# Starting the first gated head inside the last state-space group, and reordering the state steps of every group

## The reference, cut to what matters

```
xs, bm, cm = silu(dwconv(xbc))                       # state-space branch: 4 groups of 8 heads, 2 directions
y  = ssd_scan(xs, dt, a, bm, cm) + xs * d_skip       # chunks of 128 tokens: diagonal part + carried states
ys = rms_norm(y * silu(z), g_ssm_norm)               # norm over one group of 512 columns

lb = softmax(hg_lb)[0]                               # gated branch: 8 heads, 2 directions
log_f = log(lb + (1 - lb) * sigmoid(f));  k = (1 - lb) * sigmoid(-f);  q = silu(q)
o  = gla_scan(q, k, v, log_f)                        # cumulative gates, intra-chunk products, carried states
oh = rms_norm(o, g_hg_norm) * silu(og)

mixed = sigmoid(gm) * (ys @ w_branch_ssm) + sigmoid(gh) * (oh @ w_branch_hg)
```

## Time and profile before

| | |
|---|---|
| median of 3 runs | 2017.88 us (2017.27 to 2020.76) |
| profiled execution, its own time | 2020.66 us |
| its span | 2018.3 us |
| PE busy | 1781.8 us (88%) |
| DVE, ACT, POOL busy | 729.9, 449.8, 397.5 us |
| granted TensorE clock, mean | 0.955 of full speed |

### The profile page before, as it was taken

One profiled execution on the slowest core, in us unless ns is written; L12 is line 12 of the kernel. 1 busy time (PEld: TensorE's weight loads), 2 busy tenths in 40 slices (PEclk: granted clock), 3 DMA queues, 4 the chain that ended last, 5 costly groups with the idle time before them and its releaser, 6 DMA issues.

```text
span 2018.3 us, 18573 instructions
## 1 busy us (share of the span) xinstructions
PE 1781.8 (88%) x7064; PEld 963.0 (48%) x7064; DVE 729.9 (36%) x1148; ACT 449.8 (22%) x716; POOL 397.5 (20%) x464
## 2 busy tenths in 40 slices
PE   6899999999996999999999999998478878777782
PEld 1455555555554777677765444443423323333330
DVE  1534635455345665556665322124400000000003
ACT  2231231413224443434443000002110000000001
POOL 0103223141317443354441000000010000000000
PEclk9999999999998999999999999999589989899996
DMA  7212321322320111111132725212679999999993
GB/s 278 81 34 78 122 56 45 112 57 68 94 63 22 52 42 42 52 39 44 42 104 87 257 94 187 94 60 89 264 289 428 431 429 430 430 429 429 430 404 153
DMA packets 153554, 350.25 MB, mean 174 GB/s; under 512 B 14065, under 2 KB 104394, under 8 KB 140442
## 3 DMA queue, kind: packets, MB, share of 16 engines
q1 hardware_dynamic: 135962, 325.34, 42.8%
q10 hardware_dynamic: 12496, 15.75, 2.3%
q0 software_dynamic: 5040, 8.40, 1.1%
HBM read 346.09 MB, written 13.32 MB: 178 GB/s over the span
## 4 chain that ended last, share of the span: by engine, by line
PE 71%; DMA 19%; DVE 4%; POOL 3%; issue 2%; ACT 1%; SPq 0%; ACTq 0%; POOLq 0%; DVEq 0%
PE bank L498 10%; PE bank L709 10%; PE bank L747 6%; PE bank L2186 5%; PE bank L1702 5%; PE bank L1279 4%; PE bank L503 4%; DMA arena<-in_w_up_dram 3%; DMA stay<-in_w_up_dram 3%; DMA stay<-in_w_gate_dram 3%; PE bank L1704 3%; PE bank L1721 3%; PE bank L2204 3%; PE bank L494 3%; PE bank L1315 2%
## 5 line engine op out<-in xcount | busy, mean ns | idle before, releaser
L709 PE MATMUL bank<-stay,arena 128*128 128x512 f32 (+1 forms) x704 | 242.7, 501 | 9.9 <-DVE arena L934 7.7
L2186 PE MATMUL bank<-arena 128*64 128x512 f32 x832 | 201.3, 640 | 51.2 <-DMA arena<-in_w_up_dram 35.1
L709 PEld LDWEIGHTS bank<-stay,arena 128*128 128x128 f32 x704 | 133.5, 192 | 111.4 <-issue 101.3
L498 PE MATMUL bank<-arena 128*128 128x512 f32 x384 | 169.0, 593 | 1.5 <-ACT stay L610 1.5
L2186 PEld LDWEIGHTS bank<-arena 128*64 128x64 f32 x832 | 70.9, 147 | 180.1 <-issue 178.5
L2248 DVE TENSOR_TENSOR arena<-arena,bank 128x512 f32<-128x512 f32 x17 | 11.7, 688 | 325.8 <-PE bank L2186 325.8
L747 PE MATMUL bank<-arena,stay 128*128 128x512 f32 x256 | 114.0, 596 | 1.4 <-DVE arena L973 1.4
L1158 POOL TENSOR_TENSOR arena<-arena 128x256 f32<-128x256 f32 x112 | 86.6, 773 | 131.7 <-DVE arena L1472 117.5
L498 PEld LDWEIGHTS bank<-arena 128*128 128x128 f32 x384 | 71.7, 190 | 85.4 <-issue 85.4
L1471 DVE TENSOR_TENSOR arena<-arena 128x256 f32<-128x256 f32 x112 | 63.5, 607 | 132.0 <-ACT arena L1214 100.6
L2101 POOL DMA_INDIRECT y_dram<-arena x17 | 17.1, 1008 | 445.1 <-DVE arena L2255 444.5
(11 more groups left out here) (372 smaller groups left out, 2678.4 us busy)
## 6 DMA issues: line engine op xcount, KB each, us to landing
arena<-in_w_gate_dram SPq DMA_DIRECT2D x26, 2048.0 KB, 25.5
arena<-in_w_up_dram SPq DMA_DIRECT2D x26, 2048.0 KB, 26.9
arena<-in_w_down_dram SPq DMA_DIRECT2D x24, 2048.0 KB, 27.5
arena<-in_w_in_dram SPq DMA_DIRECT2D x58, 512.0 KB, 3.9
arena<-in_w_ada_dram SPq DMA_DIRECT2D x12, 2048.0 KB, 10.9
stay<-in_w_down_dram SPq DMA_DIRECT2D x10, 2048.0 KB, 26.0
stay<-in_w_gate_dram SPq DMA_DIRECT2D x8, 2048.0 KB, 25.7
stay<-in_w_up_dram SPq DMA_DIRECT2D x8, 2048.0 KB, 28.2
```

The source lines that it names most:

```text
L498: mm = pe.matmul(b[:, :], w[:, k, :], src[:, k, 0:LAT], start=(k == 0), stop=(k == KT - 1))
L709: mm = pe.matmul(ps[:, 0:n], w[:, k, :], hT[:, k, o:o + n], start=(k == 0), stop=(k == KT - 1))
L2186: mm = pe.matmul(b[cols, :], xgT[r][:, k, cols], w[u][:, k, :], start=(k == 0), stop=(k == KT - 1))
```

## The change

It has four parts.

1. **Every group.** POOL makes decayed x k = 3 ahead of exponents 3, 4 ahead of 4, and so on. State 9 moves from step 7 to step 6 on PE, and the two halves of the z projection (`gate(g, 3)`) now stand one ahead of state 8 and one ahead of state 9. In step 7 `off` 4 and 5 stand ahead of the diagonal.
2. **Groups 0 and 1.** ACT issues the two transfers of B and C weights (L422, L423) behind the last two x copies (L599), not ahead of them.
3. **Last group and head 0.** The bounds (`lower_bounds`, `lower_bound_terms`, `bounds`) move from the start of the gated branch into DVE's steps 0 and 5, ACT's exponential of them into step 3. ACT runs head 0's gates (`head_gates`) once the last diagonal is done, ahead of y's squares. PE runs units 0 and 1 of head 1 ahead of `turn_y` and unit 2 behind it. POOL starts the masks after the last `off`. Buffers are laid out anew so that nothing overlaps: the bounds get 69 columns of their own.
4. **Head bodies.** Head 0 is written out ahead of the loop; in it unit 3 stands behind level 0, and units 0 to 2 are gone (they ran before). In the other heads unit 1 moves from behind the key transposes to ahead of them, the wait for y's copies moves to those transposes, POOL does both end differences behind level 0's subtractions, and ACT does both end exponentials behind `rstd` and copies unit 1 ahead of the keys.

```diff
-        STATES = [(0,), (1, 2), (), (3, 4), (5,), (6, 7), (8,), (9,)]
+        STATES = [(0,), (1, 2), (), (3, 4), (5,), (6, 7), (8, 9), ()]
...
+        def head_gates(act, h, before):
+            act.wait_ge(s_pev, START + 8 * h + 5)
+            act.wait_ge(s_b, START + 2 * h)
+            for d in range(2):
+                act.activation(lf[d], pf[d], ACT.Sigmoid)
+            if before is not None:
+                output_sigmoid(act, before)
+            act.wait_ge(s_lw, START + NL * h)
+            for d in range(2):
+                act.activation(kh[d], pf[d], ACT.Sigmoid, scale=-1.0).then_inc(s_sg, 1)
+            act.activation(qh, pq, ACT.Sigmoid).then_inc(s_sg, 1)
+            act.preload_act_table_set(LOG_EXP)
+            act.wait_ge(s_lbh, h + 1)
+            act.wait_ge(s_sg, 4 * h + 3)
+            for d in range(2):
+                act.activation(lf[d], lf[d], ACT.Ln, scale=omlh[:, d:d + 1], bias=lbh[:, d:d + 1]).then_inc(s_ln, 1)
+
+        def output_sigmoid(act, h):
+            act.wait_ge(s_pev, START + 8 * h + 6)
+            act.wait_ge(s_q, h + 1)
+            act.activation(sog, pog, ACT.Sigmoid).then_inc(s_sg, 1)
...
+                decayed(3)
                 exponents(3)
-                for h in range(3, HG):
-                    if h < HG - 1:
-                        exponents(h + 1)
-                    for k in STATES[h]:
-                        decayed(k)
+                decayed(4)
+                exponents(4)
+                decayed(5)
+                exponents(5)
+                decayed(6)
+                decayed(7)
+                exponents(6)
+                decayed(8)
+                exponents(7)
+                decayed(9)
 
...
+                            if last and (h, part) == (3, 0):
+                                act.wait_ge(s_lbd, 1)
+                                act.activation(lbt[:, :], lbt[:, :], ACT.Exp).then_inc(s_lbe, 1)
...
+                    act.wait_ge(s_yd, START + HG * G)
+                    head_gates(act, 0, None)
                 for cc in range(LCH):
                     act.wait_ge(s_yz, START + 4 * g + cc + 1)
                     ins = act.activation(zs[:, cc, :], yt[:, cc, :], ACT.Square, accum_out=ssq[:, cc:cc + 1])
+                    if last and cc == 1:
+                        head_unit_copy(act, 0, 6)
                 ins.then_inc(s_ysum, 1)
-                act.preload_act_table_set(LOG_EXP)
+                if not last:
+                    act.preload_act_table_set(LOG_EXP)
                 act.wait_ge(s_ysum, 2 * g + 1)
...
+                    x_rows(g + 1, range(4, NCH))
                     if g + 2 < G:
                         bc_weights(act, g + 2)
-                    x_rows(g + 1, range(4, NCH))
...
-                    head_unit_copy(act, 0, 6)
                     head_unit_copy(act, 0, 7)
+                    head_unit_copy(act, 1, 0)
+                    head_unit_copy(act, 1, 1)
...
-                        if h > 2:
-                            gate(g, h // 2)
-                        for k in STATES[h]:
+                        for i, k in enumerate(STATES[h]):
+                            gate(g, h // 2, (i,) if h == 6 else (0, 1))
...
-                        state(g, 9)
                         off(g, 4)
+                        off(g, 5)
                         diagonal(g, h)
-                        for i in range(5, 8):
-                            off(g, i)
+                        off(g, 6)
+                        off(g, 7)
...
+                    head_unit(pe, 1, 0)
+                    head_unit(pe, 1, 1)
                     turn_y(g, True)
+                    head_unit(pe, 1, 2)
...
+                if last:
+                    lower_bounds(dve, own)
                 for h in range(1, HG - 1):
+                    if last and h == 5:
+                        lower_bound_terms(dve, own)
+                        bounds(dve, own, 0)
...
-            pool.wait_ge(s_yt, START + 16)
-            pool.wait_ge(s_yn, 16)
+            pool.wait_ge(s_yo, START + 8 * G)
...
+                    pool.wait_ge(s_yt, START + 4 * G)
...
-                end_differences(0)
                 pool.wait_ge(s_b, START + 2 * h + 2)
                 for i in range(NL):
                     if i == 1:
+                        end_differences(0)
                         end_differences(1)
...
-                end_exps(h, 0)
                 level_exp(h, 0)
                 if not first:
                     act.wait_ge(s_vc, h)
                     head_unit_copy(act, h, 7)
                     rstd(h - 1)
+                end_exps(h, 0)
...
-                if not last:
+                if first:
+                    head_unit_copy(act, h + 1, 2)
+                elif not last:
                     head_unit_copy(act, h + 1, 0)
+                    head_unit_copy(act, h + 1, 1)
                 else:
                     gate_copy(0, 0)
                     gate_copy(0, 1)
                 key_copies(h)
-                if not last:
-                    head_unit_copy(act, h + 1, 1)
                 level_exp(h, 2)
-                if not last:
+                if last:
+                    gate_copy(1, 0)
+                elif not first:
...
-            def body(h, last):
-                unit(h, last, 0)
+            def body(h, first, last):
+                if not first:
+                    unit(h, last, 0)
...
+                unit(h, last, 3 if first else 1)
+                if last:
+                    early_gate(pe, 1, 0, 0)
+                pe.wait_ge(s_ys, START + 4 * G)
...
-                unit(h, last, 1)
-                if last:
-                    early_gate(pe, 1, 0, 0)
                 level(h, 1)
-                unit(h, last, 2)
+                if not first:
+                    unit(h, last, 2)
```

More of the change, by code:

```diff
@@ L884, in ssd_tensor, with lower_bounds, lower_bound_terms, bounds @@
                 group(g)
+        def lower_bounds(dve, own):
+            a0, a1 = cols1[:, R_LB:R_LB + 16], cols1[:, R_LB + 16:R_LB + 32]
+            own.link(dve.tensor_tensor(lb, a0, a1, ALU.max))
+            own.mark(dve.tensor_tensor(lbt[:, 0:16], a0, lb, ALU.subtract))
+            dve.tensor_tensor(lbt[:, 16:32], a1, lb, ALU.subtract).then_inc(s_lbd, 1)
+        def lower_bound_terms(dve, own):
+            dve.wait_ge(s_lbe, 1)
+            own.wait()
+            own.link(dve.tensor_tensor(oml, lbt[:, 0:16], lbt[:, 16:32], ALU.add))
+            own.link(dve.reciprocal(oml, oml))
+            own.link(dve.tensor_tensor(lb, lbt[:, 0:16], oml, ALU.mult))
+            own.mark(dve.tensor_scalar(lb, lb, F_MIN, None, ALU.max))
+            own.mark(dve.tensor_tensor(oml, lbt[:, 16:32], oml, ALU.mult))
+            own.link(dve.tensor_copy(ghg, cols1[:, R_GHG:R_GHG + 1]))
+        def bounds(dve, own, h):
+            dve.wait_ge(s_ln, START + 2 * h)
+            own.mark(dve.tensor_copy(lbh, lb.rearrange("p (d h) -> p h d", d=2)[:, bass.ds(h, 1), :].rearrange("p a b -> p (a b)")))
+            dve.tensor_copy(omlh, oml.rearrange("p (d h) -> p h d", d=2)[:, bass.ds(h, 1), :].rearrange("p a b -> p (a b)")).then_inc(s_lbh, 1)
         def ssd_vector(dve, own):
@@ L1004, in group @@
                     weight(h + 1)
+                    if h == 6:
+                        keep_state(9)
                     if h % 2:
@@ L1349, in body @@
                 level(h, 2)
-                unit(h, last, 3)
+                if not first:
+                    unit(h, last, 3)
                 if last:
@@ L1495, in body @@
                 if not last:
-                    bounds(h + 1)
+                    bounds(dve, own, h + 1)
                 merge(0)
@@ L1533, in body @@
                     modulation_terms(dve, own, 0)
-            bounds(0)
             keys(0)
```

72 lines of the change are left out of this document (15 added, 57 removed).

## The result

| | before | after |
|---|---|---|
| median | 2019.32 us (2017.27 to 2021.93, 4 runs) | 1998.3 us (1996.2 to 2000.74, 4 runs) |
| ratio | | 0.9896, 95% interval 0.9877 to 0.9914 |
| profiled execution, span | 2018.3 us | 1993.7 us |
| granted clock, mean | 0.955 | 0.957 |
| unit 6 of head 0 starts | 596.24 us | 584.38 us |

The change makes the kernel 21.0 us faster, and 28.8 were forecast: 1989.1 us (1985.5 to 1996.5) against 1998.3 measured. The time lies outside the range. The mixer is 26.0 us shorter in the profiled pair, and the whole 24.6.

What follows compares the result with a forecast made beforehand. PE's row in the mixer was taken as the bound, its holes as all there is to win: 9.5 + 3.1 + 0.8 + 16.9 - 1.5 = 28.8 us off 2017.9 gives 1989.1 us, range 1985.5 to 1996.5.

Steps and rivals of the forecast that it cites:

- Decayed x, 9.5 us: Groups: PE's eight waits for decayed x, 7.9 us, plus 0.2 us start-up each, vanish; 9.5 us gained.
- State 9, 3.1: Step 6 of the groups: PE's waits for DVE's keeping of states shrink, with start-ups 3.1 us gained.
- the two transfers, 0.8: `turn_y`, where ACT issues two transfers ahead of its copies: 0.4 us saved, twice, 0.8 us.
- So the hole counts in full: Groups: no wait stands directly behind the removed ones, PE waits only 0.2 us at the z projection; 9.5 us kept.
- My own sign of being wrong: Listed as proof of error: gate(3) of a group, in the z projection, waiting over 0.5 us for DVE.
- The front, 16.9 us: Unit 6 to level 3 of head 0: 20.0 us over pure work vanish, 3.1 us of new wait; 16.9 us gained.
- The new hole ahead of level 2: Head 0: level 2's operand needs 4.1 us of hand-overs, level 1 covers 0.9; PE waits 3.1 us.
- the slow matmuls behind the 13 us hole: Front of head 0: matmuls after the hole ahead of level 0 ran slowly, 2.8 us together, counted as gain.
- The loop's debt, 1.5 us: Heads 1 to 6: level 1 waits for the later merge of the first product, 0.25 us each, 1.5 in all.
- The mixer, 28.8 us: Sum of all terms over groups, front and loop: the mixer gets 28.8 us shorter.
- the rivals: Full loop debt 1993.5 us (0.13), late front 1993 (0.13), groups without gain 2001.5 (0.08), slower 2030 (0.02), no change (0.02).
- So I take the gain off the median: Whole kernel: 28.8 us come off the median 2017.9, not off the profiled execution's time, 2.8 us above it.

Runs made afterwards that it cites:

- `pool_order`: Kernel before with one edit, GpSimd makes each decayed x ahead of the exponents of its step; 2012.21 us, ratio 0.9964.
- `states_only`: Kernel before with the rest of parts 1 and 2 (state 9 in step 6, transfers behind copies), GpSimd's order as before; 2020.12 us, ratio 0.9996.
- `best2`: Changed kernel; head 0's unit 3 between levels 1 and 2, first product merged first, GpSimd's exponents 5, 7 and 0 behind VectorE's steps; 1987.87 us.
- `warm`: Changed kernel with seven unread matmuls in the hole ahead of level 2 of head 0; 1995.97 us, ratio 0.9883.
- `again`: The changed kernel timed once more, unedited, in five rounds beside the kernel before; 1996.59 us, ratio 0.988.
- `fill`: Changed kernel with head 0's unit 3 between levels 1 and 2 instead of behind level 0; 1993.39 us, ratio 0.9868.
- `apart`: Changed kernel with GpSimd's exponents 5 waiting in every group until VectorE has multiplied weight 4; 1996.23 us, ratio 0.988.

## Why the prediction was wrong, by its own steps

- **Decayed x, 9.5 us**: right for what it removes (9.4 in `pool_order`). That full amount probably had luck in it: all six meetings of that trace went VectorE's way. **State 9, 3.1, and the two transfers, 0.8**: 2.6 for both together in `states_only`, where one new wait of 0.93 is in it; `turn_y` of group 1 takes 1.91 us (385.40) instead of 2.30, as forecast.
- **"So the hole counts in full"** is the first step that failed. Removing the waits is worth 14.0 us in `best2`, but the changed kernel gets 10.1 to 11.8: 1.5 to 3.2 us go into new waits for VectorE's `add_off`. My own sign of being wrong came true, the last quarter of a group's z projection waiting over 0.5 us for VectorE (0.83 at 217.93). I had worked out that VectorE's chain ends just when PE wants it, and gave it 0.2 us. What I did not do is ask when GpSimd's exponents would now run: they used to start 1.0 us after the weight (194.19 against 193.17 in group 0), and now start together with it in that very chain. I applied the lock of VectorE and GpSimd to the loop, where it costs nothing, and not to the groups, where it costs up to 3.2 us. The starting point counts too: against the profile of before unit 6 stands 11.9 us earlier, of which 1.2 us had come about before the groups began.
- **The front, 16.9 us**: 14.5. Level 0 had its cover as worked out (operand at 613.8, PE at 615.8, 2.0 us in hand). The new hole ahead of level 2 was right in place and close in size, 3.5 us against 3.1; what was missing is the merge of level 1 (0.7 us) that VectorE does between the operand and level 2's release. The larger error is that I took the slow matmuls behind the 13 us hole as a gain of 2.8 us and booked none behind the new one: 1.7 us by `warm`. 0.3 us of the miss are left unexplained, and in `again` the front gives only 13.5, since the slow matmuls cost 2.7 there.
- **The loop's debt, 1.5 us**: none. The merge of the first product ends at 675.77 in head 1 and level 1 starts at 676.43: 0.7 us of slack, where I had counted 2.5 less 2.1 to 2.8. The lock of the two engines did not cost PE anything here. The loops of both kernels run at 60.0 us a head; 0.4 us are lost behind level 3, of which 0.2 is a wait in the last head, and the rest no more than that distance scatters.

```profile
675.04 0.73 DVE L1502 COPY_PREDICATED arena<-ident,bank 128x512 f32<-128x512 uint32 x1
...
676.43 1.06 PE L1355 MATMUL bank<-arena 128*128 128x128 f32 x8
```

- **The mixer, 28.8 us**: 26.0 (11.9 + 14.5 - 0.4). Parts 1 and 2, the front and the loop are mis-sized, and none of the rivals came true. Two small slips of adding changed nothing: the hole is 4.1 less 0.9, 3.2 us and not 3.1, and 12.6 us less gain gives 2001.7, not 2001.5.
- **"So I take the gain off the median"**: the rest of the miss. Of 26.0 us the medians kept 21.0, and 23.4 on repetition. I took the 2.8 us between the profiled time and the median for mere scatter of one execution, and allowed the end of the expert stage nothing, though it differs by up to 4.1 us between executions. The median of before itself moved from 2017.88 to 2019.32 with a fourth run, and stood at 2020 in the later sets: the start was low. Adding 2.8 for the mixer and 1.4 for the start gives 1993.3, inside the range; the other 5.0 us up to 1998.3 are of the size of the steps in the table, but only 1.4 of them are seen in the profiled pair. Nor does the table explain the 2.8 us: the profiled execution of before has one of the short stages (539.5).

What stays open is why long stages are more frequent in some kernels: seven of eleven executions of `states_only` are 3.7 to 4.6 us above its fastest, though its mixer is 3.8 us shorter than before. The waits and slow sets fit the order of the stages in the profiled executions; that they make the other executions' times as well is argued, not shown.

## What to carry to other kernels

When a wait of GpSimd is taken away, work out when its instructions run afterwards and which two-input instruction of VectorE they meet; a wait of GpSimd for VectorE's step brought no new wait of PE here and gave back 2.1 to 3.9 us of the groups. A hole on TensorE costs its length and may cost the slow matmuls behind it as well, so filler goes where the hole is, and the engine that releases the next step does that release first. A gain far ahead of a stage bound by transfers arrives, but less or more the few microseconds by which that stage's end varies, so read it at the end of its own stage. And one trace without a wait is weak evidence where the order of two starts decides it: count the meetings, not only the waits.

## What the runs showed of the hardware

- Which of two starts within 0.15 us comes first decides whether VectorE's 0.69 us instruction takes 0.69 or 1.45 to 1.58 us, and with it whether PE waits 0.7 to 0.9 us: 16 of 42 meetings in seven executions, the places varying between executions of one program.
- Behind an idle stretch of TensorE of 3.52 us the granted clock was 0.59 for 4 us; behind one of 3.29 us, one level earlier in the same head (`fill`), it stayed at 1.00. In the expert stage the set behind a wait of 3.58 us took 7.09 us in `again` and 8.78 in `apart`. The length of the hole alone doesn't decide.
- Where PE waits for a transfer anyway, slow matmuls ahead of that wait cost nothing, and behind it 1.7 to 2.7 us a set: the six executions with two sets of 8.78 us ahead of the last `up` weights have the six shortest stages of the 14.
- Unread matmuls that fill a hole bring back in speed most of what they overrun: 2.3 us late at the hole's end, 0.6 us late 3 us further on, against the execution with the cheaper hole.
